# Two transformer blocks in one fp32 kernel: the opening stage and the first norm put into one block, with two of four modulation blocks as products on TensorE

## The chip, the cores and the metric

## What is computed

Two transformer blocks run one behind the other on a sequence of 512 tokens of width 1024; the second has 256 context tokens beside them. Only the opening matters here:

```python
c_act = jax.nn.silu(c)
mod = (c_act @ w_ada[l] + b_ada[l])[:, None, :]           # 1 x 1024 times 1024 x 6144
sh_m, sc_m, ga_m, sh_f, sc_f, ga_f = jnp.split(mod, 6, axis=-1)
h = _rms_norm(x, g_pre_mix[l]) * (1.0 + sc_m) + sh_m
y = _hybrid_mixer(h, ...)                                 # opens with proj = h @ w_in

def _rms_norm(x, g):
    y = xf * lax.rsqrt(jnp.mean(xf * xf, axis=-1, keepdims=True) + EPS)
    return (y * g).astype(x.dtype)
```

The first norm needs the shift `sh_m` and the scale `sc_m`, the first 2048 of the 6144 columns: four blocks of 512, numbered 0 to 3.

## The kernel before

`build` runs five stages in turn. Instructions are written out by hand for each engine in blocks (`nc.Block()`), each engine runs its list in the order in which it is written, and a block ends with a barrier of all engines. Within a block, semaphores alone order the engines.

Activations are held with the features on the 128 partitions: `K.x[:, k, ...]` is feature group k of 8 (`KT`), with 256 context tokens and then 512 tokens. Weights come through `K.ring`, three slots of 2 MB, in a fixed order (`weight_items`): the w_ada blocks 0, 1, 2, 3, then the query weights (`nq`, eight pieces), the key weights (`kv`), and so on. SP issues the load of an item once the item three places before has been left, that is, once the semaphore named in `ring.left` has its value.

**`stage_start`** loads constants, tokens and context on SP's queue and 20 rows of small parameters on ACT's. PE turns the parameters (line 393), then the tokens and the context in alternation, 8 feature groups each (line 402; four transposes for the tokens, two for the context), into four banks. DVE copies every bank to `K.x` (line 344). Then come the four modulation blocks: `modulation_sums` on DVE multiplies each of 8 tiles of 128x512 weights by its column of silu(c) and adds (lines 439 and 441), which leaves one 128x512 tile of partial sums; `modulation_columns` on PE adds over the partitions, with 128 columns of that tile as the stationary side and a column of ones moving (line 467), four matmuls a block, straight into the columns of bank 7 in which the rest wants them. Lines 349 and 352 on DVE make shift and scale.

**`rms_norms`**, called at the top of `stage_mixer_1`, is a block of its own: ACT loads its table and squares the 8 groups (line 500) into two buffers, PE sums each over the partitions with a matrix of ones (line 523), ACT takes Ln and Exp (lines 505, 506), DVE multiplies by the root (line 542) into two buffers, and ACT applies scale and shift (line 512) to give `K.h`.

**`project_1`** is the next block. PE multiplies `K.h` by the query weights (line 823), with the sums for the context's norm (line 832) and rotations (line 796) between; SP loads first three halves of the second block's modulation weights and then the next item of the ring.

## Time and profile before

| | |
|---|---|
| median of 3 runs | 2465.08 us (2464.07 to 2465.39) |
| profiled execution, its time | 2464.89 us |
| profiled execution, its span | 2463.1 us |
| PE busy, share of the span | 2300.7 us, 93% |
| DVE busy | 1036.7 us, 42% |
| ACT busy | 484.0 us, 20% |
| POOL busy | 693.3 us, 28% |
| DMA, mean over the span | 102 GB/s |

The span is what the trace covers, from the first instruction to the last; the profiled execution's own time is 1.8 us more. Times in the trace count from the start of the span. The granted clock is 1.00 at 2.4 GHz and 0.50 at 1.2 GHz. A row of the timeline may stand for several instructions (x8): its duration then runs from the first one's start to the last one's end.

### The profile page before, as it was taken

The numbers are of one execution on the slowest core, as the hardware profiler recorded it, in microseconds if no ns is written. First come the engines' busy times: TensorE is split into PE (matmuls) and PEld (weight loads), VectorE is DVE, ScalarE is ACT, GpSimd is POOL, SyncE is SP. The second block draws the span as 40 slices with busy tenths as digits, with TensorE's granted clock in tenths as the row PEclk, the third lists the DMA queues.
The fourth block names the chain that finished last, engine by engine and source line by source line (L and its number), as shares of the span: only waits on it lengthen the run. The fifth ranks groups of instructions, "written<-read, shape, count | busy, mean of one in ns | idle before, by whom it ended". The sixth has DMA issues, their size and how long they took to land. (4 is left out here: it accounts for less than half of the span.)

```text
span 2463.1 us, 26565 instructions
## 1 busy us (share of the span) xinstructions
PE 2300.7 (93%) x10463; PEld 1790.6 (73%) x10463; DVE 1036.7 (42%) x1913; ACT 484.0 (20%) x1110; POOL 693.3 (28%) x549
## 2 busy tenths in 40 slices
PE   4899897889999899999989999997999899999998
PEld 2454576667776788888878888885556668888887
DVE  5555386443342763235453322452433422112354
ACT  1201122223342200101130011113132532000002
POOL 0000000000001355556245555640010103555552
PEclk7999697889999999999989999998999999999999
DMA  8632432543341245223234522231121121222230
GB/s 278 207 112 103 135 103 74 181 143 95 95 138 51 86 157 185 74 66 93 94 102 137 186 88 71 71 116 44 34 73 69 35 69 43 95 91 70 71 93 36
DMA packets 255271, 250.14 MB, mean 102 GB/s; under 512 B 19858, under 2 KB 207404, under 8 KB 255020
## 3 DMA queue, kind: packets, MB, share of 16 engines
q1 hardware_dynamic: 254712, 248.30, 32.1%
q8 instruction: 84, 1.38, 0.2%
q14 instruction: 39, 0.32, 0.0%
q10 hardware_dynamic: 436, 0.15, 0.0%
HBM read 243.19 MB, written 4.19 MB: 100 GB/s over the span
## 5 line engine op out<-in xcount | busy, mean ns | idle before, releaser
L1917 POOL TENSOR_TENSOR w_sums<-ring 128x512 f32<-128x512 f32 x66 | 91.7, 1389 | 528.5 <-POOLq L1249 355.7
L1933 POOL TENSOR_TENSOR hidden<-rstd,h_act 128x256 f32<-128x256 f32 x66 | 53.9, 816 | 434.6 <-DVE h_act L2110 434.6
L823 PE MATMUL ps<-h_act,ring 128*128 128x512 f32 (+1 forms) x288 | 129.7, 605 | 9.5 <-PEq L487 8.7
L1802 PE MATMUL ps<-h_sums,w_sums 128*128 128x256 f32 x528 | 128.5, 387 | 10.6 <-DVE h_sums L2046 10.6
L2110 DVE TENSOR_TENSOR h_act<-ps,rstd 128x256 f32<-128x256 f32 x78 | 33.0, 424 | 233.2 <-PE ps L1820 136.6
L1820 PE MATMUL ps<-h_sums,ring 128*128 128x256 f32 x528 | 125.8, 381 | 3.1 <-DVE rstd L2089 3.1
L1808 PE MATMUL ps<-h_act,ring 128*128 128x256 f32 x528 | 126.9, 384 | 0.0
L1767 PE MATMUL ps<-h_act,ring 128*128 128x256 f32 x528 | 125.2, 381 | 0.0
L1814 PE MATMUL ps<-h_sums,w_sums 128*128 128x256 f32 x528 | 124.8, 379 | 0.2 <-DVE rstd L2082 0.2
L1825 PE MATMUL ps<-h_act,w_sums 128*128 128x256 f32 x528 | 124.7, 379 | 0.0
L1775 PE MATMUL ps<-h_act,ring 128*128 128x256 f32 x528 | 124.5, 379 | 0.0
L2082 DVE TENSOR_TENSOR rstd<-ps,h_act 128x256 f32<-128x256 f32 x78 | 33.1, 425 | 212.5 <-PE ps L1802 176.1
L1802 PEld LDWEIGHTS ps<-h_sums,w_sums 128*128 128x128 f32 x528 | 102.2, 194 | 26.0 <-issue 11.7
L1615 PE MATMUL ps<-h_act,ring 128*128 128x256 f32 (+1 forms) x384 | 113.3, 455 | 4.5 <-PEq L2452 3.9
L1820 PEld LDWEIGHTS ps<-h_sums,ring 128*128 128x128 f32 x528 | 99.5, 190 | 20.3 <-DVE rstd L2089 7.2
L1808 PEld LDWEIGHTS ps<-h_act,ring 128*128 128x128 f32 x528 | 102.1, 193 | 14.5
L1814 PEld LDWEIGHTS ps<-h_sums,w_sums 128*128 128x128 f32 x528 | 100.2, 190 | 14.2 <-DVE rstd L2082 0.6
L1775 PEld LDWEIGHTS ps<-h_act,ring 128*128 128x128 f32 x528 | 100.1, 190 | 14.3 <-issue 0.8
L1825 PEld LDWEIGHTS ps<-h_act,w_sums 128*128 128x128 f32 x528 | 100.3, 190 | 13.6
L823 PEld LDWEIGHTS ps<-h_act,ring 128*128 128x128 f32 (+1 forms) x288 | 53.8, 189 | 77.5 <-issue 77.2
L1767 PEld LDWEIGHTS ps<-h_act,ring 128*128 128x128 f32 x528 | 99.4, 190 | 13.0
L1615 PEld LDWEIGHTS ps<-h_act,ring 128*128 128x128 f32 x384 | 73.4, 192 | 42.0 <-issue 35.3
(443 smaller groups left out, 4456.3 us busy)
## 6 DMA issues: line engine op xcount, KB each, us to landing
ring<-in_ffn_w_in SPq DMA_DIRECT2D x66, 1024.0 KB, 7.7
ring<-in_w_ada SPq DMA_DIRECT2D x12, 2048.0 KB, 8.5
ring<-in_w_mod SPq DMA_DIRECT2D x12, 2048.0 KB, 8.0
ring<-in_w_gate_up SPq DMA_DIRECT2D x22, 1024.0 KB, 8.1
ring<-in_ffn_w_out SPq DMA_DIRECT2D x32, 704.0 KB, 5.8
ring<-in_w_in SPq DMA_DIRECT2D x6, 2048.0 KB, 8.1
ring<-in_ffn_w_out SPq DMA_DIRECT2D x8, 1408.0 KB, 7.1
ring<-in_w_down SPq DMA_DIRECT2D x16, 704.0 KB, 6.4
```

Of the source, the lines that this page charges most:

```text
L823: last = pe.matmul(K.ps[i % 3][0:rows, :], lhs(w, item, j, k), hl(k), start=(k == 0), stop=(k == KT - 1))
L1615: last = pe.matmul(K.ps[i % 3][:, 0:b - a], w[:, k, (d % 4) * P:(d % 4) * P + P], K.h[:, k, CTX + a:CTX + b], start=(k == 0), stop=(k == K ...
L1767: last = pe.matmul(pa, a11[:, k], F.h11[:, k], start=(k == 0), stop=(k == 3))
L1775: last = pe.matmul(pa, a12[:, k], F.h21[:, k], start=False, stop=(k == 3), skip_group_check=True)
L1802: last = pe.matmul(pb, s2[:, k], F.t2[:, k], start=(k == 0), stop=(k == 3))
L1808: last = pe.matmul(pc, a21[:, k], F.h12[:, k], start=(k == 0), stop=(k == 3))
L1814: last = pe.matmul(pb, s1[:, k], F.t1[:, k], start=(k == 0), stop=(k == 3))
L1820: last = pe.matmul(pc, a22[:, k], F.t4[:, k], start=False, stop=(k == 3), skip_group_check=True)
L1825: last = pe.matmul(pb, s4[:, k], F.h22[:, k], start=False, stop=(k == 3), skip_group_check=True)
L1917: pool.tensor_tensor(s1, a21, a22, ALU.add).then_inc(S["wsum"].sem, 1)
L1933: pool.tensor_tensor(one[:, j], F.gate1[f % 2], F.got21[f % 2], ALU.mult)
L2082: dve.tensor_tensor(F.v, pb, F.kept1[u % 2], ALU.add).then_inc(S["v"].sem, 1)
```

## The change

`stage_start` and the first norm become one block, and `rms_norms` with its helpers goes.

- SP loads the tokens in two halves, then modulation block 0, then the context.
- PE turns the tokens alone, then sums the squares for the norm, then turns the context. DVE copies the turned tokens as before; ACT copies the context.
- ACT squares each group of `K.x` as soon as it is copied. Ln and Exp follow the sums.
- Blocks 1 and 3 are products on PE (`product`): the column of silu(c) is the stationary side, 128x1, the weights 128x512 are the moving side, 8 matmuls add up one row of 512. ACT copies the row to SBUF, and four matmuls with one partition (`columns`) turn it into columns. Blocks 0 and 2 stay with DVE.
- DVE multiplies `K.x` by the root into `K.h` between its two blocks; ACT applies scale and shift in place.
- The counts of `K.mod_mm` follow, since only two blocks now pass through it (`MODS_START`). In later stages some semaphores are shared (`K.out_mm`) or left out where nothing uses them. Apart from the names of these semaphores the order on every engine behind this block is as before, and POOL's list does not change.

PE behind the last block of columns, before. `sq` is the tile that DVE leaves, `ones` a matrix of ones, line 523 the sum of the squares, line 823 the first projection:

```order
L467 MATMUL ps<-ones,sq 128x1 [waits mod_sum]
L467 MATMUL ps<-ones,sq 128x1 x3
L327 UNCONDITIONAL_BRANCH
L516 UNCONDITIONAL_BRANCH [waits barrier_Pool_Activation_PE_DVE_SP_release]
L523 MATMUL ps<-sq,ones 128x512 [waits norm_sq] x8
L487 UNCONDITIONAL_BRANCH
L787 UNCONDITIONAL_BRANCH [waits barrier_Pool_Activation_PE_DVE_SP_release]
L823 MATMUL ps<-h_act,ring 128x512 [waits ring_filled1]
```

After, PE from the end of the context's transposes to the last columns. `cc` is silu(c); `rstd` and `sq` hold the copied rows in line 429; line 533 is `modulation_columns`:

```order
L421 MATMUL ps<-ring,cc 1x512 [waits ring_filled1,silu_done]
L421 MATMUL ps<-ring,cc 1x512 x7
L533 MATMUL ps<-ones,sq 128x1 [waits mod_sum]
L533 MATMUL ps<-ones,sq 128x1 x3
L429 MATMUL ps<-ones,rstd 128x1 [waits st_row_kept]
L429 MATMUL ps<-ones,rstd 128x1 x3
L421 MATMUL ps<-ring,cc 1x512 [waits ring_filled0]
L421 MATMUL ps<-ring,cc 1x512 x7
L429 MATMUL ps<-ones,sq 128x1 [waits st_row_kept]
L429 MATMUL ps<-ones,sq 128x1 x3
L533 MATMUL ps<-ones,sq 128x1 [waits mod_sum]
L533 MATMUL ps<-ones,sq 128x1 x3
```

Two barriers between columns and projection have become one, the sums of the squares have moved ahead (they stand before the context's transposes), and two products stand between the columns, the second queued behind the columns of the first.

DVE from the fourth modulation block to the norm's multiplications, before:

```order
L439 TENSOR_SCALAR sq<-ring,cc 128x512 [waits mod_mm,ring_filled0]
L441 SCALAR_TENSOR_TENSOR sq<-ring,cc,sq 128x512 [waits dve_step] x7
L349 TENSOR_TENSOR mod<-ps,par 128x16 [waits mod_mm]
L352 SCALAR_TENSOR_TENSOR coef<-mod,par 128x8 [waits x_kept]
L327 UNCONDITIONAL_BRANCH
L526 UNCONDITIONAL_BRANCH [waits barrier_Pool_Activation_PE_DVE_SP_release]
L542 TENSOR_TENSOR tmp<-x_res,rstd 128x512 [waits norm_std]
L542 TENSOR_TENSOR tmp<-x_res,rstd 128x512
L542 TENSOR_TENSOR tmp<-x_res,rstd 128x512 [waits norm_out] x6
```

After, DVE from the copies of the tokens to the coefficients:

```order
L346 COPY x_res<-ps 128x512 [waits x_turned] x8
L505 TENSOR_SCALAR sq<-ring,cc 128x512 [waits ring_filled0,silu_done]
L507 SCALAR_TENSOR_TENSOR sq<-ring,cc,sq 128x512 [waits dve_step] x7
L351 TENSOR_TENSOR h_act<-x_res,rstd 128x512 [waits st_root]
L351 TENSOR_TENSOR h_act<-x_res,rstd 128x512 x7
L505 TENSOR_SCALAR sq<-ring,cc 128x512 [waits ring_filled2]
L507 SCALAR_TENSOR_TENSOR sq<-ring,cc,sq 128x512 [waits dve_step] x7
L355 TENSOR_TENSOR mod<-ps,par 128x16 [waits mod_mm,st_row_cols]
L358 SCALAR_TENSOR_TENSOR coef<-mod,par 128x8 [waits st_coef]
```

Two of the four sums are gone, the context's copies are gone, the multiplications by the root stand between the two sums that are left, and the coefficients wait for `st_row_cols` as well.

```diff
@@ -72,6 +72,7 @@
+MODS_START = 2
...
@@ -317,9 +319,13 @@
-    const_in, param_in, x_in = K.sem("const_in"), K.sem("param_in"), K.sem("x_in")
+    const_in, param_in, x_in = K.sem("const_in"), K.sem("param_in"), [K.sem(f"x_in{i}") for i in range(3)]
     set_done, par_t, par_done = K.sem("set_done"), K.sem("par_t"), K.sem("par_done")
-    turned, kept, silu_done = K.sem("x_turned"), K.sem("x_kept"), K.sem("silu_done")
+    turned, kept, ctx_kept, silu_done = K.sem("x_turned"), K.sem("x_kept"), K.sem("ctx_kept"), K.sem("silu_done")
+    squared, summed, log, root, normed, row_mm, row_kept, row_cols, coef = (K.sem(f"st_{n}") for n in (
+        "squared", "summed", "log", "root", "normed", "row_mm", "row_kept", "row_cols", "coef"))
+    rows = [K.rstd[0:1, 1, :], K.sq[0:1, 0, :]]
+    rstd = K.rstd[:, 0, :]
     with ExitStack() as st:
...
@@ -335,22 +341,22 @@
                 for g in range(3):
                     dve.wait_ge(par_t, g + 1)
                     dve.tensor_copy(K.par[g][:, :], K.ps[g][:, 0:PCOL[g]]).then_inc(par_done, 1)
-                for k in range(0, KT):
-                    for part in range(2):
-                        i = 2 * k + part
-                        dve.wait_ge(turned, i + 1)
-                        dst = K.x[:, k, CTX:TOK] if part == 0 else K.x[:, k, 0:CTX]
-                        src = K.ps[3 + i % 4][:, 0:SEQ if part == 0 else CTX]
-                        dve.tensor_copy(dst, src).then_inc(kept, 1)
+                for k in range(KT):
+                    dve.wait_ge(turned, k + 1)
+                    dve.tensor_copy(K.x[:, k, CTX:TOK], K.ps[3 + k % 4][:, :]).then_inc(kept, 1)
                 dve.wait_ge(silu_done, 1)
-                for n in range(4):
-                    modulation_sums(K, dve, ("ada", n))
-                dve.wait_ge(K.mod_mm, 4)
-                dve.tensor_tensor(K.mod1[:, 0:16], K.ps[7][:, 0:16], K.p("b_ada", 0, 16), ALU.add).then_inc(kept, 1)
-                dve.wait_ge(kept, 2 * KT + 1)
+                modulation_sums(K, dve, ("ada", 0))
+                dve.wait_ge(root, 1)
+                for k in range(KT):
+                    dve.tensor_tensor(K.h[:, k, CTX:TOK], K.x[:, k, CTX:TOK], rstd, ALU.mult).then_inc(normed, 1)
+                modulation_sums(K, dve, ("ada", 2))
+                dve.wait_ge(row_cols, 2)
+                dve.wait_ge(K.mod_mm, 2)
+                dve.tensor_tensor(K.mod1[:, 0:16], K.ps[7][:, 0:16], K.p("b_ada", 0, 16), ALU.add).then_inc(coef, 1)
+                dve.wait_ge(coef, 1)

                 dve.scalar_tensor_tensor(K.coef[:, 0], K.mod1[:, 8:16], 1.0, K.p("g_pre_mix"), ALU.add,
-                                         ALU.mult).then_inc(kept, 1)
+                                         ALU.mult).then_inc(coef, 1)

             @block.scalar
             def _(act):
@@ -383,33 +389,93 @@
                 act.activation(K.cc1[:, :], K.p("c"), ACT.Silu)
                 act.activation(K.cc2[:, :, 0], K.p("c_2"), ACT.Silu)
                 act.activation(K.cc2[:, :, 1], K.p("c_ctx_2"), ACT.Silu).then_inc(silu_done, 1)
+                act.preload_act_table_set(LOG_EXP)
+                for k in range(KT):
+                    act.wait_ge(kept, k + 1)
+                    if k >= 2:
+                        act.wait_ge(summed, k - 1)
+                    act.activation(K.tmp[:, k % 2, :], K.x[:, k, CTX:TOK], ACT.Square).then_inc(squared, 1)
+                act.wait_ge(summed, KT)
+                act.activation(rstd, K.ps[0][:, :], ACT.Ln, bias=K.eps[:, 0:1], scale=1.0 / D).then_inc(log, 1)
+                act.wait_ge(log, 1)
+                act.activation(rstd, rstd, ACT.Exp, scale=-0.5).then_inc(root, 1)
+                for k in range(KT):
+                    act.wait_ge(turned, KT + k + 1)
+                    act.activation(K.x[:, k, 0:CTX], K.ps[3 + k % 4][:, 0:CTX], ACT.Copy).then_inc(ctx_kept, 1)
+                for i in range(2):
+                    act.wait_ge(row_mm, i + 1)
+                    if i == 1:
+                        act.wait_ge(K.mod_mm, 1)
+                    act.activation(rows[i], K.ps[1 + i][0:1, :], ACT.Copy).then_inc(row_kept, 1)
+                act.wait_ge(coef, 2)
+                act.wait_ge(normed, KT)
+                for k in range(KT):
+                    h = K.h[:, k, CTX:TOK]
+                    act.activation(h, h, ACT.Identity, bias=K.mod1[:, k:k + 1], scale=K.coef[:, 0, k:k + 1])

             @block.tensor
             def _(pe):
+                def product(n, i):
+                    w = K.ring.take(pe, ("ada", n)).rearrange("p (k n) -> p k n", k=KT)
+                    for k in range(KT):
+                        last = pe.matmul(K.ps[1 + i][0:1, :], K.cc1[:, k:k + 1], w[:, k, :], start=(k == 0),
+                                         stop=(k == KT - 1))
+                    last.then_inc(row_mm, 1)
+                    K.ring.left(row_mm, i + 1)
+
+                def columns(n, i):
+                    pe.wait_ge(row_kept, i + 1)
+                    for c in range(4):
+                        last = pe.matmul(K.ps[7][:, 4 * n + c:4 * n + c + 1], rows[i][:, c * P:c * P + P],
+                                         K.ones[0:1, 0:1], start=True, stop=True)
+                    last.then_inc(row_cols, 1)
+
                 pe.wait_ge(const_in, 16)
                 pe.wait_ge(param_in, 16 * n_params)
                 for g in range(3):
                     n = PCOL[g]
                     pe.transpose(K.ps[g][:, 0:n], prow[0:n, g, :], const(K, "ident")[0:n, 0:n]).then_inc(par_t, 1)
-                pe.wait_ge(x_in, 32)
+                pe.wait_ge(x_in[0], 16)
+                pe.wait_ge(x_in[1], 16)
                 for k in range(KT):
-                    for part in range(2):
-                        i = 2 * k + part
-                        if i >= 4:
-                            pe.wait_ge(kept, i - 3)
-                        src = xr if part == 0 else cr
-                        for t in range(QT if part == 0 else CC):
-                            last = pe.transpose(K.ps[3 + i % 4][:, t * P:t * P + P], src[:, t, k * P:k * P + P],
-                                                const(K, "ident"))
-                        last.then_inc(turned, 1)
-                for n in range(4):
-                    modulation_columns(K, pe, ("ada", n))
+                    if k >= 4:
+                        pe.wait_ge(kept, k - 3)
+                    for t in range(QT):
+                        last = pe.transpose(K.ps[3 + k % 4][:, t * P:t * P + P], xr[:, t, k * P:k * P + P],
+                                            const(K, "ident"))
+                    last.then_inc(turned, 1)
+                pe.wait_ge(set_done, 1)
+                pe.wait_ge(par_done, 3)
+                for k in range(KT):
+                    pe.wait_ge(squared, k + 1)
+                    pe.matmul(K.ps[0][:, :], K.ones[:, :], K.tmp[:, k % 2, :], start=(k == 0),
+                              stop=(k == KT - 1)).then_inc(summed, 1)
+                pe.wait_ge(x_in[2], 16)
+                for k in range(KT):
+                    if k < 4:
+                        pe.wait_ge(kept, 5 + k)
+                    else:
+                        pe.wait_ge(ctx_kept, k - 3)
+                    for t in range(CC):
+                        last = pe.transpose(K.ps[3 + k % 4][:, t * P:t * P + P], cr[:, t, k * P:k * P + P],
+                                            const(K, "ident"))
+                    last.then_inc(turned, 1)
+                pe.wait_ge(silu_done, 1)
+                product(1, 0)
+                modulation_columns(K, pe, ("ada", 0))
+                columns(1, 0)
+                product(3, 1)
+                columns(3, 1)
+                modulation_columns(K, pe, ("ada", 2))

             @block.sync
             def _(sp):
                 sp.dma_start(K.cst[:, :], A["consts"]).then_inc(const_in, 16)
-                sp.dma_start(xr[:, :, :], A["x"][0].rearrange("(t p) d -> p t d", p=P)).then_inc(x_in, 16)
-                sp.dma_start(cr[:, :, :], A["ctx_2"][0].rearrange("(t p) d -> p t d", p=P)).then_inc(x_in, 16)
+                x = A["x"][0].rearrange("(t p) d -> p t d", p=P)
+                for i in range(2):
+                    sp.dma_start(xr[:, 2 * i:2 * i + 2, :], x[:, 2 * i:2 * i + 2, :]).then_inc(x_in[i], 16)
+                K.ring.load_ahead(sp, ("ada", 0))
+                sp.dma_start(cr[:, :, :], A["ctx_2"][0].rearrange("(t p) d -> p t d", p=P)).then_inc(x_in[2], 16)
                 K.ring.load_ahead(sp, "kv")

...
@@ -470,97 +536,11 @@
-def rms_norms(K, jobs):
...
 def stage_mixer_1(K, out):
-    rms_norms(K, [norm_in(lat(K.x), SEQ, K.coef[:, 0], K.mod1[:, 0:8], lat(K.h))])
...
@@ -904,14 +884,14 @@
-                    dve.wait_ge(K.mod_mm, 4 + 4)
+                    dve.wait_ge(K.mod_mm, MODS_START + 4)
...
@@ -1592,7 +1572,7 @@
-    O.mm = K.sem(f"po_mm{call}")
+    O.mm = Tally(K.out_mm, call * len(OUT_PIECES))
```

## Rows read from the trace of the kernel before

**Rows 1.** Timeline: start us, us, engine line op; in brackets idle before and releaser

```profile
14.29 1.11 PE L402 MATMUL ps<-cst,x_rows 128*128 128x128 f32 x4 [0.26 <-DMA ctx_rows<-in_ctx]
...
15.44 1.02 DVE L344 COPY x_res<-ps 128x512 f32<-128x512 f32 x2 [1.16 <-PE ps L402]
...
16.90 0.87 PE L402 MATMUL ps<-cst,x_rows 128*128 128x128 f32 x4
...
17.82 0.60 PE L402 MATMUL ps<-cst,x_rows 128*128 128x128 f32 x4
...
21.83 0.38 PE L402 MATMUL ps<-cst,ctx_rows 128*128 128x128 f32 x2
...
23.91 5.48 DVE L441 SCALAR_TENSOR_TENSOR sq<-ring,cc,sq 128x512 f32<-128x512 f32 x7
```

**Rows 2.** Timeline, the four modulation blocks and the coefficients

```profile
29.30 0.48 DVE L439 TENSOR_SCALAR sq<-ring,cc 128x512 f32<-128x512 f32 x1
...
35.32 10.07 SPq L237 DMA_DIRECT2D ring<-in_w_in  x10
...
47.16 1.86 PE L467 MATMUL ps<-ones,sq 128*128 128x1 f32 x8 [4.04 <-DVE sq L441]
...
49.27 0.17 DVE L352 SCALAR_TENSOR_TENSOR coef<-mod,par 128x8 f32<-128x8 f32 x1
```

**Rows 3.** Timeline, the norm and the start of the first projection

```profile
51.70 9.13 PE L523 MATMUL ps<-sq,ones 128*128 128x512 f32 x16 [2.68 <-ACT sq L500]
...
58.04 0.63 ACT L500 ACTIVATE sq<-x_res 128x512 f32<-128x512 f32 x1 [0.23 <-PE ps L523]
...
59.03 0.63 ACT L500 ACTIVATE sq<-x_res 128x512 f32<-128x512 f32 x1 [0.35 <-PE ps L523]
...
60.87 0.69 ACT L505 ACTIVATE rstd<-ps,eps 128x512 f32<-128x512 f32 x1 [1.22 <-PE ps L523]
...
62.98 6.24 ACT L512 ACTIVATE h_act<-tmp,mod,coef 128x512 f32<-128x512 f32 x8 [0.76 <-DVE tmp L542]
...
69.52 10.06 PE L823 MATMUL ps<-h_act,ring 128*128 128x512 f32 x16 [8.69 <-PEq L487]
```

**Rows 4.** Timeline of PE later in the first projection

```profile
178.47 0.28 PE L467 MATMUL ps<-ones,sq 128*128 128x1 f32 x2
...
180.17 7.11 PE L823 MATMUL ps<-h_act,ring 128*128 128x512 f32 x16
...
230.16 7.04 PE L823 MATMUL ps<-h_act,ring 128*16 128x512 f32 x16
```

**Rows 5.** Windows: us, busy of each engine (records), PEclk (granted clock), DMA share, GB/s

```profile
24.00:26.00 2.00, 0.00 (x0) 0.00 (x0) 1.93 (x3) 0.00 (x0) 0.00 (x0) 0.57 1.06 389
...
54.00:56.00 2.00, 2.00 (x4) 0.48 (x2) 0.00 (x0) 1.07 (x2) 0.00 (x0) 0.75 0.00 0
...
230.00:237.20 7.20, 7.20 (x20) 1.68 (x19) 4.19 (x7) 0.00 (x0) 0.00 (x0) 1.00 0.69 262
...
257.00:273.00 16.00, 15.77 (x16) 4.00 (x16) 4.10 (x6) 1.88 (x4) 0.00 (x0) 0.50 0.94 269
...
283.20:286.60 3.40, 3.40 (x34) 3.40 (x32) 2.49 (x4) 0.00 (x0) 0.00 (x0) 1.00 0.00 0
...
286.60:290.00 3.40, 3.40 (x20) 3.40 (x20) 0.16 (x1) 0.31 (x1) 0.00 (x0) 0.57 0.89 287
```

**Rows 6.** Groups by form: line engine op shapes xcount, busy us, mean ns, idle before

```profile
L344 DVE COPY x_res<-ps 128x512 f32<-128x512 f32 x8 | 5.5, 688 | 1.5 <-PE ps L402 1.4
...
L542 DVE TENSOR_TENSOR tmp<-x_res,rstd 128x512 f32<-128x512 f32 x8 | 5.4, 691 | 13.5 <-ACT rstd L506 12.8 <-ACT h_act L512 0.6
...
L684 ACT ACTIVATE rstd<-ps 128x256 f32<-128x256 f32 x8 | 3.1, 383 | 24.6 <-PE ps L645 24.6
```

**Rows 7.** Line 237, the loads of the ring, issued in 29 to 35 us

```profile
L237 SPq DMA_DIRECT2D ring<-in_w_ada x1: 368/368/368, 29.4 to 29.4; - x1
...
DMA to landing us min/median/max: 8.0/8.0/8.0
```

More of the change, by code:

```diff
@@ L292, in build @@
         K.mods_summed = K.mods_turned = 0
-        K.norm_sems = {n: Tally(nc.alloc_semaphore(f"norm_{n}")) for n in ("sq", "mm", "std", "tmp", "out")}
+        K.norm_sems = {n: Tally(nc.alloc_semaphore(f"norm_{n}")) for n in ("sq", "mm", "std", "tmp")}
+        K.out_mm = nc.alloc_semaphore("out_mm")
         K.fast = {n: nc.alloc_semaphore(f"fast_{n}") for n in FAST_COUNTS}
@@ L1400, in coefs_1 @@
 def coefs_1(K, dve, done):
[L1402 removed]
+    dve.wait_ge(K.mod_mm, MODS_START + 8 + MODS_FIRST)
     dve.tensor_tensor(K.mod1[:, 16:48], K.ps[7][:, 16:48], K.p("b_ada", 16, 32), ALU.add).then_inc(done, 1)
@@ L1417, in coefs_2 @@
     m = K.ps[7][:, 48:192].rearrange("p (j v) -> p j v", v=2)
-    dve.wait_ge(K.mod_mm, 12 + MODS_FFN[call][-1] + 1)
+    dve.wait_ge(K.mod_mm, MODS_START + 8 + MODS_FFN[call][-1] + 1)
     n = 0
@@ L1616, in out_tensor @@
                              start=(k == 0), stop=(k == KT - 1))
-        last.then_inc(O.mm, 1)
+        last.then_inc(O.mm.sem, 1)
         if i in (3, len(OUT_PIECES) - 1):
-            K.ring.left(O.mm, i + 1)
+            K.ring.left(O.mm.sem, O.mm.base + i + 1)
         if O.context and i < 4:
@@ L1644, in out_scalar @@
     for i, (d, a, b, _) in enumerate(OUT_PIECES):
-        act.wait_ge(O.mm, i + 1)
+        O.mm.wait(act, i + 1)
         y_square(K, O.T, act, i, K.ps[i % 3][:, 0:b - a])
```

74 lines of the change are left out of this document (3 added, 71 removed).

## The prediction, made before the changed kernel was run

> **What bounds the kernel now.** I read the timeline of the first 70 us first, because the change ends there: the order of the instructions after the first projection is the same on every engine, so whatever the first projection gains in its start is the whole gain, unless the clock at that start differs. The reader should see three things. First, DVE is the bound from 15.4 us on: it copies the turned tokens and then sums four blocks of w_ada back to back, 5.9 us each (three of them from 29.30 to the 47.16 at which PE gets the last) [rows 1, 2], while PE only turns each finished sum into columns (1.86 us) and ACT is idle. Second, the tail is serial: last columns end 49.02, coefficients end 49.44 [rows 2]. Third, the norm starts only then, although its squares need nothing but x, which was in place before 23.9: squares and their sums on PE to 60.83, Ln and Exp to 62.22 (the 62.98 less the 0.76 of idle), then eight scalings on ACT to 69.22, and the first projection matmul at 69.52 [rows 3]. That is 20.1 us behind the coefficients, of which only the last 6.24 depend on them.
>
> **What the change removes, and the new chain.** I build the new start of the projection, T', from rows, and compare it with 69.52. Every engine is followed; PE turns out last.
>
> 1. Tokens alone are turned now: PE starts at 14.03 (the 14.29 less the 0.26 it waited for the context) [rows 1]. At first twelve transposes take 14.29 to 16.90, 0.87 for a group of four; at the fast level a group is done in 0.60 with its drain (17.82) [rows 1]. DVE's copy is 0.69 [rows 6] and starts 1.15 behind the first transpose: 15.2. The third copy waits for PE until 14.03 + 3 x 0.87 + 0.3 = 16.95, the rest run back to back at 0.70, so the fourth ends 18.35 and the eighth 21.15. PE's last group reuses the bank of the fourth copy and ends between 18.8 and 18.95; I take 18.8, since the sum follows while it drains.
> 2. The sum over the features: 8 matmuls. Fast, the square loop steps by 0.86 to 0.99 (58.04 and 59.03; the floor is 7.04 / 8 = 0.88) [rows 3, 4]; I take 0.93, 7.4 in all: 26.2. The squares on ACT come earlier: they follow the copies, and the table load ahead of them falls into ACT's idle time.
> 3. Ln and Exp: 60.83 to 62.22, 1.4 [rows 3]: 27.6. The second table load and one block boundary of the old path are gone.
> 4. The context is turned behind the sums. Four groups go at once, the other four wait for ACT, which copies 0.38 each [rows 6] from 27.6: 27.6 + 4 x 0.38 + 0.25 = 29.4.
> 5. First product (block 1) on PE. The trace has no matmul with one stationary column. The nearest row has 16 of them and 512 moving: 8 matmuls (16 records) in 7.04, the same as with 128 [rows 4]. Since eight times fewer columns saved nothing, 7.0 is the lower end; the upper is twice that, 14.1, at the slow level. I take 7.0, the value of the nearest row: 36.4. Its weights are there: DVE began on them at 29.30 without a wait [rows 2], and the bytes queued ahead of them are unchanged.
> 6. Columns of block 0 and then of the product, four matmuls each. At the fast level eight such took 1.70 (178.47 to 180.17), at the slow one four took 1.86 [rows 2, 4]. Two sets: 1.7, 38.1. The copy of the row on ACT (0.69 as the Ln of a bank, the dearest of its kind) lies beside the first set. The products' columns have one partition as stationary depth, which no row has; bounds 0.8 and 1.9 a set.
> 7. Second product 7.0: 45.1. Its weights are issued when DVE has summed block 0 (21.15 + 5.9 = 27.05) and took 8.0 to land [rows 7]: 35.1, wanted at 38.1. That cover is 3.0.
> 8. Here nothing hides the row's copy: 0.7, then two sets 1.7: 47.5. Block 2, which DVE summed, is queued behind the second product's columns.
> 9. The two small operations for the coefficients: 49.02 to 49.44, 0.4: 47.9.
> 10. Eight scalings 6.24 and the boundary 0.30 (69.22 to 69.52) [rows 3]: 54.45. For some eight handoffs between engines, 0.02 to 0.05 each, I add 0.4: **T' = 54.9**.
>
> The other engines are early: DVE multiplies by the root eight times at 0.69 [rows 6] from 27.6 to 33.2, sums block 2 to 39.1, and PE asks for it at 46.7. On SP the query weights wait for the first product, now 36.4 instead of 35.3; all ten issues, the keys' included, take 10.1 [rows 2], and even the 8.0 of a 2 MB load behind the last gives 54.5 [rows 7]; the query's pieces are the first eight, so they are in before 54.9. Splitting the load of x in two and putting block 0 ahead of the context change no byte that PE waits for before 14.03; the context is wanted at 26.2 and was there at 14.29 [rows 1]; with 2 MB more ahead of it, it comes at most 8.0 later [rows 7]. Renamed semaphores and shared counters cost nothing.
>
> So the projection starts 69.52 - 54.9 = 14.6 earlier. Its own first group ran slow, 10.06 against 7.04 [rows 3, 4], behind 8.7 of idle PE; now PE idles 7.4 before it, and I expect the same 3.0 to be lost (if the level stayed high instead, 3.0 more would be gained). The profiled execution of 2464.89 then becomes 2450.3; the median of the runs is 0.2 above it: **2450.4**.
>
> **A rule against the change.** Of transposes the rows show that four took 1.11 at first and 0.60 from 17.82 on, though nothing but transposes had run since 14.29 [rows 1]: PE reached its fast level on them. The Trainium skill (TensorE: Matmul & The Clock Gate, Part 4: PE-mode transpose) says that the full clock does not engage in transpose mode, since it does not count as PE-busy in the same way. By that rule the sums would open at the slow level. Worked out from rows, that mechanism gives: transposes at 0.87 a group to 21.0, the sums in 9.13 as they took after an idle PE [rows 3], ending 30.1 instead of 26.2, so 2454.3. The trace disagrees with the rule, so it gets little.
>
> **Rivals.** All hang on the level of PE's clock, since 24.8 us of the new chain (sums 7.4, products 14.0, columns 3.4) are PE work that doubles at 1.2 GHz, where before DVE's sums did not care.
>
> *The level falls in the context gap* (26.2 to 29.4, where PE has 16 transposes and an idle stretch of 0.9). For: after the last transposes at 21.83 the granted clock fell, 0.57 from 24 to 26 [rows 1, 5]. Against: there the idle stretch went on, here it is short, and the last transposes before, each pair held up by DVE's copies, still took 0.38 for two [rows 1]. Price: 1.7 (9.13 less 7.4 for the sums) to 3.0 (first projection group) [rows 3, 4]: 2452.1 to 2453.4, say 2452.8.
>
> *One stationary column does not hold the level.* For: a busy PE is not enough. Matmuls of one moving column kept it busy 3.40 of 3.40 and the level fell right behind, 1.00 to 0.57; and with 16 of 128 rows in every second matmul PE was busy 15.77 of 16.00 and stayed at 0.50 [rows 5]. Against: 16 stationary columns, busy for 7.04, held 1.00 through 230.0 to 237.2 [rows 5]; the moving side there is as full as in the products. Price: product 29.4 to 43.5, two sets 3.7, product to 61.3, copy 0.7, two sets to 65.7, then 0.4, 6.24, 0.3 and 0.4: T' = 73.1. That would be 2468.5; with the first of it still fast, 2466.8. I put it at 2468.
>
> *The slow level from the first transpose to the last column*, the case on the other side. Transposes to 21.0, sums 14.1 to 35.1, 8.9 later than forecast, then the products as above: T' = 82.0, 2477. It decides from the point where 14.6 of the 24.8 us of PE work are lost; for 0.2% beyond, 19.5. Against: in the kernel before these same sums, from 51.70 on, raised the level by themselves: 0.75 over 54 to 56 [rows 3, 5].
>
> **How the numbers follow.** Forecast 0.56; level lost in the gap 0.23; transposes as by the rule 0.03; products slow 0.14; slow throughout 0.04. The range takes in the first three (0.82): down to 2447.4 if the projection opens fast, up to 2456 for the rule's case with the higher bounds of the columns and handoffs. A measurement of this kernel tells about 0.2%, 4.9 us, from no change: faster (below 2460.1) is the first three, 0.82; same holds the products at the slow level, 0.14; slower 0.04.
>
> **What would show it.** In the profile after: sums start near 18.8 and end near 26.2; each product has 16 records of 0.59 (1.1 if slow) and lasts 7.0; granted clock 1.00 from 17 to 47; the scalings start near 48 and follow the last columns, not DVE; the first projection matmul is at 54.9, with its first group near 10.1. I am wrong if a window between 26 and 47 shows 0.50, if PE waits for block 3 at 38, or if the projection waits for its weights.

## The result, and the profile after

The changed kernel took 2445.7 us (median of 4 runs, 2443.27 to 2448.42) beside 2464.57 us of the kernel before on the same chip: a ratio of 0.9927, 95% interval 0.9913 to 0.9942. It is faster by 18.9 us, where 14.6 was forecast, and the median lies 1.7 us below the low end of the range. The profiled execution took 2447.78 us, its span is 2446.0.

The timeline of the start (start us, duration us, engine, line, operation, tiles, count; in brackets the idle time before and what ended it) answers to [rows 1 to 3]:

```profile
13.66 5.51 PE L444 MATMUL ps<-cst,x_rows 128*128 128x128 f32 x32
...
17.37 3.08 DVE L346 COPY x_res<-ps 128x512 f32<-128x512 f32 x5 [0.16 <-PE ps L444]
19.01 7.61 PE L451 MATMUL ps<-tmp,ones 128*128 128x512 f32 x16
...
26.66 0.69 ACT L399 ACTIVATE rstd<-ps,eps 128x512 f32<-128x512 f32 x1 [1.22 <-PE ps L451]
...
28.33 1.26 PE L460 MATMUL ps<-cst,ctx_rows 128*128 128x128 f32 x8 [0.84 <-ACT x_res L404]
...
29.52 7.03 PE L421 MATMUL ps<-ring,cc 128*1 128x512 f32 x16
...
36.48 1.05 PE L533 MATMUL ps<-ones,sq 128*128 128x1 f32 x8
...
37.46 1.05 PE L429 MATMUL ps<-ones,rstd 1*128 1x1 f32 x8
...
38.44 7.03 PE L421 MATMUL ps<-ring,cc 128*1 128x512 f32 x16
...
45.51 0.59 ACT L409 ACTIVATE sq<-ps 1x512 f32<-1x512 f32 x1 [8.33 <-PE ps L421]
...
48.28 0.17 DVE L355 TENSOR_TENSOR mod<-ps,par 128x16 f32<-128x16 f32 x1 [9.43 <-PE ps L533]
48.49 0.17 DVE L358 SCALAR_TENSOR_TENSOR coef<-mod,par 128x8 f32<-128x8 f32 x1
48.69 5.74 ACT L414 ACTIVATE h_act<-h_act,mod,coef 128x512 f32<-128x512 f32 x8 [2.60 <-DVE coef L358]
...
54.73 8.90 PE L803 MATMUL ps<-h_act,ring 128*128 128x512 f32 x16 [6.56 <-PEq L333]
...
63.90 7.03 PE L803 MATMUL ps<-h_act,ring 128*128 128x512 f32 x16
```

PE now carries the block: it has work nearly without a gap from 13.66 to 48.17, and DVE, the bound of before, waits 9.4 us for it ahead of the coefficients. The norm's root is there at 28.0, 20 us before the coefficients. Windows of the same stretch (busy time of PE, PEld, DVE, ACT, POOL with the number of records, then granted clock, DMA share, GB/s) show the clock that the prediction hung on:

```profile
17.00:26.00 9.00, 9.00 (x33) 4.38 (x32) 8.59 (x14) 3.80 (x7) 0.00 (x0) 1.00 1.04 396
26.00:30.00 4.00, 3.16 (x20) 1.87 (x19) 2.32 (x5) 3.31 (x10) 0.00 (x0) 1.00 1.05 387
30.00:36.00 6.00, 6.00 (x16) 1.13 (x14) 5.86 (x10) 0.20 (x1) 0.00 (x0) 1.00 0.89 326
...
45.00:48.00 3.00, 2.32 (x18) 1.84 (x16) 0.00 (x0) 0.59 (x1) 0.00 (x0) 1.00 1.28 240
48.00:50.00 2.00, 0.17 (x2) 0.09 (x1) 0.34 (x2) 1.31 (x2) 0.00 (x0) 0.53 1.05 369
```

The granted clock is 1.00 (2.4 GHz) from the transposes to the last columns, through the context gap of 26 to 30 too; in this profile it falls to 1.2 GHz only where PE waits for the scalings, 0.53 and then 0.50.

So the projection starts at 54.73 instead of 69.52 [rows 3], 14.8 earlier. But the spans differ by 2463.1 - 2446.0 = 17.1, and the medians by 18.9. The experiments ask two things: whether the start gained for the reasons given, and where the rest comes from.

### The profile page after: what moved, and what is told of

The parts are those of the page before. It is cut to its first block and busy times, and to the rows that moved or that the text cites. A ratio compares the mean times of both kernels' runs of the same rounds, so it can differ in the third digit from the quotient of the medians.

```text
span 2446.0 us, 26616 instructions
## 1 busy us (share of the span) xinstructions
PE 2311.3 (94%) x10495; PEld 1793.0 (73%) x10495; DVE 1022.4 (42%) x1889; ACT 487.1 (20%) x1120; POOL 689.9 (28%) x549
## 5 line engine op out<-in xcount | busy, mean ns | idle before, releaser
L1782 PEld LDWEIGHTS ps<-h_sums,w_sums 128*128 128x128 f32 x528 | 103.3, 196 | 26.4 <-issue 11.7
L1800 PEld LDWEIGHTS ps<-h_sums,ring 128*128 128x128 f32 x528 | 99.5, 190 | 19.5 <-DVE rstd L2069 6.4
L1788 PEld LDWEIGHTS ps<-h_act,ring 128*128 128x128 f32 x528 | 102.9, 195 | 14.9
```

Of the source, the lines that this page charges most:

```text
L1782: last = pe.matmul(pb, s2[:, k], F.t2[:, k], start=(k == 0), stop=(k == 3))
L1788: last = pe.matmul(pc, a21[:, k], F.h12[:, k], start=(k == 0), stop=(k == 3))
L1800: last = pe.matmul(pc, a22[:, k], F.t4[:, k], start=False, stop=(k == 3), skip_group_check=True)
```

## The experiments

Two theories about the rest. By the first, the gain at the start is passed on rigidly, and what is beyond it is the scatter of single runs. By the second, moving the start changes where behind it the clock falls and rises, and this gives or takes a few microseconds by itself. All comparisons are with the kernel before on the same chip.

**One half alone: the norm beside the transposes, all four blocks summed on DVE.** From the changed kernel, `product(1, 0)` and its like are left out of PE's program and DVE sums all blocks:

```diff
                 for k in range(KT):
                     dve.tensor_tensor(K.h[:, k, CTX:TOK], K.x[:, k, CTX:TOK], rstd, ALU.mult).then_inc(normed, 1)
-                modulation_sums(K, dve, ("ada", 2))
+                for n in range(1, 4):
+                    modulation_sums(K, dve, ("ada", n))
...
```

> The changed kernel with all four modulation blocks summed on VectorE, none as a product; the norm stays in the block. By the rows of the changed kernel: block 0 is summed by 26.3, the multiplications by the root end 32.9, three more sums of 5.95 end 50.7, columns at the slow level 1.9, coefficients 0.45, scalings 5.75 and boundary 0.3: projection at 59.1. If the rival is right that the merged norm alone brings the gain and the products nothing, it starts at 54.7. Forecast 59.1, time 4.4 above the changed kernel's, less than the spread of single runs.

Measured: 2455.79 us (8 runs), ratio 0.9960, interval 0.9946 to 0.9973; mean 2454.0. Its timeline:

```profile
50.74 1.87 PE L524 MATMUL ps<-ones,sq 128*128 128x1 f32 x8 [4.04 <-DVE sq L498]
...
53.06 5.74 ACT L409 ACTIVATE h_act<-h_act,mod,coef 128x512 f32<-128x512 f32 x8 [22.84 <-DVE coef L358]
...
59.10 10.16 PE L794 MATMUL ps<-h_act,ring 128*128 128x512 f32 x16 [6.49 <-PEq L333]
```

PE gets the last sum 3.6 later than before (47.16, [rows 2]), since DVE now also multiplies by the root. But nothing stands behind the coefficients but the scalings: the projection starts 10.4 earlier. The idle time of 4.04 ahead of the columns says that DVE is still the bound. The start of 59.10 is the one forecast, and the rival by which the products bring nothing falls with it; the time is not: the mean is 9.1 us above the changed kernel's, where 4.4 was expected.

**The other half alone: two products on PE, the norm where it was.** The same two products and their columns, in the old block:

```diff
-                for n in range(4):
-                    modulation_sums(K, dve, ("ada", n))
-                dve.wait_ge(K.mod_mm, 4)
+                modulation_sums(K, dve, ("ada", 0))
+                modulation_sums(K, dve, ("ada", 2))
+                dve.wait_ge(row_cols, 2)
+                dve.wait_ge(K.mod_mm, 2)
...
+                product(1, 0)
+                modulation_columns(K, pe, ("ada", 0))
+                columns(1, 0)
+                product(3, 1)
+                columns(3, 1)
+                modulation_columns(K, pe, ("ada", 2))
```

> The kernel before, norm in its own block, with blocks 1 and 3 as products on TensorE. The first product starts near 25, just as the clock falls: 10 to 14 us; the second cannot start before block 3 has landed at 37.4, ends 44.5 at the fast level, columns and coefficients by 47.5; then the old norm, 20.1: projection at 67.6, a gain of 2 out of the 14.8. If products and merged norm add up, it would be 14.8 - 10.4 = 4.4.

Measured: 2461.51 us (12 runs), ratio 0.9986, interval 0.9976 to 0.9997; mean 2461.2. That is at most a small gain. Its timeline shows where it goes:

```profile
25.26 8.72 PE L402 MATMUL ps<-ring,cc 128*1 128x512 f32 x16 [2.58 <-DMA ring<-in_w_ada]
29.87 0.37 SPq L238 DMA_DIRECT2D ring<-in_w_ada  x1
...
37.99 7.03 PE L402 MATMUL ps<-ring,cc 128*1 128x512 f32 x16 [2.05 <-DMA ring<-in_w_ada]
...
50.46 10.36 PE L555 MATMUL ps<-sq,ones 128*128 128x512 f32 x16 [2.73 <-ACT sq L532]
...
60.86 0.69 ACT L537 ACTIVATE rstd<-ps,eps 128x512 f32<-128x512 f32 x1 [1.22 <-PE ps L555]
...
69.52 9.10 PE L850 MATMUL ps<-h_act,ring 128*128 128x512 f32 x16 [8.70 <-PEq L519]
```

PE waits for weights twice, 2.58 for block 1 and 2.05 for block 3, which is issued only at 29.87, when DVE has given its part of the ring back. The sums of the squares start 1.2 earlier than in [rows 3] and take 10.36 instead of 9.13, with more of them at the slow level, so that the Ln stands where it stood, at 60.86 against 60.87. Products alone are hidden behind the weights and the clock. The gain of 2 at the start that was expected is 0.0 against [rows 3] (69.52 both times), and 1.1 if taken at the second group of matmuls (78.88 against 80.0, the mean of two profiles of the kernel before); the first product took 8.72, less than the 10 to 14 expected. Beside the early norm they bring 4.4 at the start of the projection (59.10 to 54.73), and 9.1 in the means (2454.0 to 2444.9, the mean of all runs of the changed kernel below).

**A product that opens cold.** The first product is made to wait until DVE has finished its second sum (`pe.wait_ge(K.mod_sum, 2)` ahead of `product(1, 0)`), so that PE stands idle for 9.4 us ahead of it:

> The changed kernel in which TensorE waits for VectorE's second sum (38.8) ahead of its first product, so that it is idle from 29.5 on and the clock falls. Does a matmul with one stationary column count? If it does not raise the level, the first product takes 14.1 and the second too, and the projection starts at about 80. If it does, the first takes 9 to 11, the second 7.0, and the projection starts at 54.7 + 9.4 + 3 = 67.

Measured: 2455.75 us, in a single run. Timeline and windows:

```profile
39.43 8.58 PE L421 MATMUL ps<-ring,cc 128*1 128x512 f32 x16 [9.36 <-issue]
...
49.90 7.03 PE L421 MATMUL ps<-ring,cc 128*1 128x512 f32 x16
```

```profile
38.00:40.00 2.00, 0.57 (x1) 0.11 (x2) 1.29 (x2) 0.00 (x0) 0.00 (x0) 0.50 0.00 0
40.00:42.00 2.00, 2.00 (x4) 0.30 (x3) 0.00 (x0) 0.00 (x0) 0.00 (x0) 0.50 0.04 8
42.00:44.00 2.00, 2.00 (x6) 0.34 (x5) 0.00 (x0) 0.00 (x0) 0.00 (x0) 0.86 0.00 0
44.00:48.00 4.00, 4.00 (x11) 0.72 (x9) 0.00 (x0) 0.00 (x0) 0.00 (x0) 1.00 0.00 0
```

The product starts at 0.50 and raises the clock itself, to 0.86 and then 1.00; the cold start cost it 1.55 (8.58 less 7.03), and the projection starts at 66.19, near the 67 of that case and far from the 80 of the other. One stationary column is enough here, both to hold and to raise the level. The first product of the kernel with the products alone says the same from a second run: 8.72 behind 2.58 of idle PE. The rival by which one column is not enough falls.

**Dummy work to hold the level.** Seven matmuls whose result nobody reads, behind the last columns of the changed kernel:

```diff
                 columns(3, 1)
                 modulation_columns(K, pe, ("ada", 2))
+                for k in range(7):
+                    pe.matmul(K.ps[0][:, :], K.ones[:, :], K.x[:, k, CTX:TOK], start=True, stop=True)
```

> The changed kernel with seven matmuls of 128x512 more on TensorE (ones times x, result unused) behind its last columns, 48.2 to about 54.2, where it was idle. The projection still starts at 54.7. R, with the clock's price taken at the start alone: the granted clock stays 1.00, the first group takes 7.1 instead of 8.9, span 2446.0 - 1.8 = 2444.2. S: the same first group, but the end moves by 0 or by 3 to 4 us, not by 1.8.

Measured: 2446.03 us (6 runs), ratio 0.9932, interval 0.9918 to 0.9946; mean 2445.6.

```profile
48.52 7.95 PE L471 MATMUL ps<-x_res,ones 128*128 128x512 f32 x14
...
56.77 7.11 PE L805 MATMUL ps<-h_act,ring 128*128 128x512 f32 x16 [0.30 <-PEq L333]
```

The first group takes 7.11 instead of 8.90: its loss does come from the idle PE ahead. But the seven took 7.95, not the 6.2 of the fast level (14 records of 0.44), and end 1.6 behind the scalings (56.47, 54.92). The projection starts 2.0 later than in the changed kernel, about what its group is shorter by. The expectation had it start at 54.7 still, and a span of 2444.2 or one moved by 0 or by 3 to 4 us; the profile's span is 2443.3 and the mean 0.7 above the changed kernel's. Nothing is won.

**The start moved by known amounts.** In the kernel before, four squarings on ACT that nobody reads are put at the end of the norm (2.3 us); in the changed kernel, two and four of them (1.15 and 2.3 us) behind the last scaling, here the four:

```diff
+            for dst in (K.sq[:, 0, :], K.sq[:, 1, :], K.rstd[:, 1, :]):
+                act.activation(dst, K.rstd[:, 0, :], ACT.Square)
+            act.activation(K.h[:, 0:2, 0:CTX], K.rstd[:, 0, :].rearrange("p (a n) -> p a n", a=2), ACT.Square)
```

```diff
+                for dst in (K.tmp[:, 0, :], K.tmp[:, 1, :], K.sq[:, 0, :], K.sq[:, 1, :]):
+                    act.activation(dst, rstd, ACT.Square)
```

> The kernel before, with four squarings of 128x512 more on ScalarE behind the norm's last scaling, 2.3 us in all, results unused; the first projection starts at 71.8 instead of 69.5. Theory R (everything behind the projection's start shifts rigidly): span 2463.1 + 2.3 = 2465.4. Theory S (the end is set by where the later falls and rises of TensorE's clock come, and work re-aligns to them): in the two traces these changes stand 17.07 us apart from 1220 us on, though the projection started only 14.8 earlier; so the first 2.3 us of that start are free, the span stays at 2463.1 within 0.5.

> The changed kernel with two squarings more on ScalarE behind the last scaling, 1.15 us; the projection starts at 55.9. R: span 2446.0 + 1.2 = 2447.2. S: the start lies then, against the clock's changes, as it did in the kernel before, so its first group of matmuls takes 10.1 again instead of 8.9 and the span is 3 to 4 us longer than 2446.0, not 1.2.

> The same with four squarings, 2.3 us; the projection starts at 57.0. R: span 2448.3. S: no more than with two, since work re-aligns to the same clock changes: equal to the run with two squarings within 0.5.

Measured: before with 2.3 more 2461.58 (12 runs; ratio 1.0001, 0.9988 to 1.0014; mean 2463.0); after with 1.15 more 2446.09 (6 runs; 0.9933, 0.9918 to 0.9949; mean 2445.9); after with 2.3 more 2443.68 (6 runs; 0.9925, 0.9909 to 0.9940; mean 2443.8). The profiles show the starts at 72.64, 56.19 and 56.72, which is 3.1, 1.5 and 2.0 later than in the first profile of each kernel. Passed on rigidly, that gives +2.3, +1.15 and +2.3. Measured, mean against mean: +0.2 (the kernel before had 2462.8 on that chip), +1.0 and -1.1 (against the 2444.9 of all runs of the changed kernel). The second theory had named 0 for the first of them, which fits, 3 to 4 for the middle one, and for the last the same as for the middle one: it misses both. The first theory misses the first by 2.1 and the last by 3.4, and fits the middle one. Each kernel's runs spread by 7 to 12 us, so that a mean of 6 is good to 2 or 3 us only: these runs exclude neither theory, and the question was put below what so few runs resolve.

**Both kernels once more.**

> The changed kernel, unedited, for more runs beside more of the kernel before. The runs so far spread over 10 us for either kernel, and a delay of 1.15 or 2.3 us did not show in their times. Theory N (the start of the projection moves by 14.8, the rest of the difference is where in each run the clock's changes fall): means apart by 14.8, within 1.5. Theory G (something behind the projection's start became faster for good): 17 or more.

> The changed kernel once more, to enlarge the sample beside the kernel before on the same chip: the mean of ten runs so far is 2445.4 against 2463.8 of the kernel before in forty, a difference of 18.3, where the projection starts 14.8 earlier. Theory N (only the start counts, the rest is the spread of the runs): the pooled difference moves toward 15 to 17. Theory G (something behind the start gives more): it stays at 18 or above.

> The kernel before once more, for a second profile of it. The changed kernel's three profiles start the projection at 54.73, 54.44 and 54.95 and its second group at 63.90, 64.8 and 64.21, so the start hardly varies, while their spans are 2446.0, 2437.7 and 2443.0. If the kernel before behaves likewise, its projection starts within 0.5 of 69.52 and its second group between 78.6 and 79.9, and what lies behind the second group varies by several us with the amount of slow level in it: the 191.5 us at the slow level behind the start that its first profile has would be found changed by 10 or more. If instead its start varies by 2 or 3, the forecast of 14.6 was anchored on a chance start, and the 3 us between the gain at the start and the gain in the mean would come from there.

Measured: the changed kernel 2445.54 (6 runs; ratio 0.9921, 0.9904 to 0.9938) and 2443.95 (6 runs; 0.9916, 0.9899 to 0.9933); the kernel before against itself 0.9999 (0.9983 to 1.0014), with runs from 2454.33 to 2469.69 us. Taken together: before 2463.4 in the mean of 80 runs (they spread with a standard deviation of 3.8), after 2444.9 in the mean of 16 (2.8): a difference of 18.5, with 1.6 of uncertainty at 95%. By the words of the two expectations for the changed kernel that is the case of something behind the start that gives more: 19.5 in the first repetition, where 14.8 within 1.5 stood against 17 or more, and 18.5 with the second, where 15 to 17 stood against 18 or above. How much more depends on what is taken for the gain at the start. The timeline of the kernel before, second profile:

```profile
52.54 9.85 PE L523 MATMUL ps<-sq,ones 128*128 128x512 f32 x16 [2.68 <-ACT sq L500]
...
71.08 8.84 PE L823 MATMUL ps<-h_act,ring 128*128 128x512 f32 x16 [8.69 <-PEq L487]
...
80.19 5.31 PE L823 MATMUL ps<-h_act,ring 128*128 128x512 f32 x12
```

What was expected of this second profile came out in neither form. The start of the projection is 1.6 later than in [rows 3], 71.08, but its first group is 1.2 shorter; the second group starts at 80.19, where 79.85 stood in the first profile. In three profiles of the changed kernel it starts at 63.90, 64.79 and 64.21. By the second groups the gain at the start is 80.0 - 64.3 = 15.7, with a scatter of 0.9 at most in either kernel. The slow level behind the start, from 90 us on, was 191.5 us in the first profile of before and is 194.9 in the second, so it did not change by the 10 or more that were expected; in the three of after it is 201.7, 177.8 and 191.5. More scatter lies behind. Two profiles of the same changed kernel, spans 2446.0 and 2437.7: in the first, an instruction on ACT that both have stands at 448.88 and a later one at 812.92,

```profile
448.88 0.38 ACT L677 ACTIVATE x_res<-ps 128x256 f32<-128x256 f32 x1 [2.61 <-PE ps L616]
...
812.92 0.42 ACT L1984 ACTIVATE h_act<-h_act 128x256 f32<-128x256 f32 x1 [13.49 <-DVE h_act L2103]
```

and in the second (a run of the same program) they stand at

```profile
445.41 0.38 ACT L677 ACTIVATE x_res<-ps 128x256 f32<-128x256 f32 x1 [1.66 <-PE ps L616]
...
804.96 0.42 ACT L1984 ACTIVATE h_act<-h_act 128x256 f32<-128x256 f32 x1 [12.56 <-DVE h_act L2103]
```

3.5 and then 8.0 us earlier, though the second had started its second group of matmuls 0.9 later. One group of PE in that stretch and windows around two short waits of PE, in the first profile:

```profile
783.72 6.22 PE L1518 MATMUL ps<-hidden,ones 128*128 128x256 f32 x16 [3.90 <-ACT hidden L1511]
...
780.00:790.00 10.00, 6.29 (x18) 5.14 (x19) 5.98 (x6) 4.96 (x9) 0.00 (x0) 0.66 0.32 103
796.00:806.00 10.00, 6.46 (x18) 4.96 (x17) 5.63 (x6) 3.40 (x6) 0.00 (x0) 0.66 0.01 2
```

and in the second, the same group and windows around the same two waits:

```profile
779.18 3.72 PE L1518 MATMUL ps<-hidden,ones 128*128 128x256 f32 x16 [3.90 <-ACT hidden L1511]
...
774.00:784.00 10.00, 6.10 (x28) 5.05 (x28) 7.01 (x7) 6.58 (x13) 0.00 (x0) 1.00 0.47 154
789.00:799.00 10.00, 6.43 (x23) 5.06 (x22) 5.71 (x7) 3.37 (x6) 0.00 (x0) 0.83 0.00 0
```

The granted clock is the third number from the right: 0.66 and 0.66 in the one, 1.00 and 0.83 in the other. The same 16 records behind the same 3.90 of idle PE take 6.22 in the one and 3.72 in the other: the clock falls in one run and not, or for less time, in the other. The runs' mean clocks go with their times: 0.957 and 0.958 at spans of 2446.0 and 2446.6, 0.962 at 2439.3 and 2439.7 (changed kernel); and in 29 runs of the kernel before on one chip 0.959 or 0.960 in the four below 2456 us, 0.951 to 0.953 in the eight of 2466 us and more.

**Can it be made faster still.** The profile of after says what is serial at the end: the second product's row copy (0.59), the columns of block 2 behind it, and eight scalings on ACT while DVE idles. The next kernel turns block 2 first and gives five of the scalings to DVE; the one after it adds three dummy matmuls behind the last columns:

```diff
                 dve.wait_ge(coef, 2)
+                dve.wait_ge(normed, KT)
+                for k in range(3, KT):
+                    h = K.h[:, k, CTX:TOK]
+                    dve.tensor_scalar(h, h, K.coef[:, 0, k:k + 1], K.mod1[:, k:k + 1], ALU.mult, ALU.add)
...
-                for k in range(KT):
+                for k in range(3):
...
                 product(3, 1)
-                columns(3, 1)
                 modulation_columns(K, pe, ("ada", 2))
+                columns(3, 1)
+                for k in range(3):
+                    pe.matmul(K.ps[0][:, :], K.ones[:, :], K.x[:, k, CTX:TOK], start=True, stop=True)
```

> The changed kernel with two more edits at the end of its first block: PE turns DVE's sum of block 2 into columns while ACT copies the second product's row, and the last scalings are shared, three on ACT and five on DVE, in place of eight on ACT. If the profile of the changed kernel is read rightly, the 0.6 of the row's copy is hidden and five scalings of 0.48 each on DVE take the place of 5.74 on ACT: the last columns end near 47.5, the coefficients near 48.0, the first projection matmul starts near 50.7 in place of 54.73, 4.0 earlier. Theory N (a start moved by so much moves the mean of many runs by so much, give or take what the clock gives back in the first group, where PE idles less): mean 4.0 less than the changed kernel, near 2441. Theory G (a gain at the start is partly given back or enlarged behind, by where the clock changes fall): the profile shows the 4.0 at the start, and the mean of the runs stands off 2441 by more than 2.

> The previous kernel with three matmuls of 512 moving columns whose result nobody reads behind the last columns, so that PE works through part of the 3.3 in which it would wait for the scalings. If the level of the first projection's first group hangs on that idle time, the group takes 7.1 to 8 in place of 8.9 to 10.1, and the mean is up to 2.5 less than that of the previous kernel, near 2439. If the level has already fallen because of the matmuls of one moving column ahead, the three run slow (5 to 5.2 in all), the projection starts some 1.5 to 2 late, and the time is equal or 1 worse.

Measured: with the shared scalings 2440.21 us (5 runs), ratio 0.9905, interval 0.9889 to 0.9921, mean 2441.1; with the dummy matmuls too 2437.10 us (5 runs), ratio 0.9891, interval 0.9875 to 0.9907, mean 2437.7. The first one's timeline:

```profile
46.26 1.05 PE L538 MATMUL ps<-ones,sq 128*128 128x1 f32 x8
46.36 0.59 ACT L414 ACTIVATE sq<-ps 1x512 f32<-1x512 f32 x1 [8.33 <-PE ps L426]
...
48.73 2.23 ACT L419 ACTIVATE h_act<-h_act,mod,coef 128x512 f32<-128x512 f32 x3 [1.79 <-DVE coef L358]
48.73 2.37 DVE L364 TENSOR_SCALAR h_act<-h_act,coef,mod 128x512 f32<-128x512 f32 x5
...
51.41 9.77 PE L808 MATMUL ps<-h_act,ring 128*128 128x512 f32 x16 [3.12 <-PEq L333]
```

and the second one's:

```profile
46.99 4.54 PE L476 MATMUL ps<-x_res,ones 128*128 128x512 f32 x6
...
51.83 7.11 PE L810 MATMUL ps<-h_act,ring 128*128 128x512 f32 x16 [0.30 <-PEq L333]
```

The row's copy now lies beside the columns of block 2, and 2.37 of scalings stand where 5.74 stood. The projection starts 3.3 earlier than at 54.73, not the 4.0 expected, because this profile's second product starts 0.9 later (its 32 transposes took 6.46, not 5.51); from the second product on, the start is 4.2 nearer. The mean, 2441.1, is the one that the first theory had named, but five runs don't settle it. The dummies took 4.54 in place of 2.7, slowed as in the experiment with seven, and end 1.6 behind the scalings (49.88, 51.5), but the first group pays that back with 2.7 (9.77 to 7.11): so the slow dummies of the one branch of the expectation came with the fast group of the other. In the two profiles the second groups start 2.3 apart (61.45 and 59.20); 1.2 of it was there before the dummies (the second product at 39.30 and 38.07), and 1.0 is the dummies' net. The 3.4 between the two means of five runs each is uncertain by 3.0 at 95%, so it doesn't say more than that. Against the changed kernel's mean of 2444.9 the last version is 7 us better, and it is the fastest kernel of this study.

## Why the prediction was wrong, and what of it was right

The mechanism at the start came out as forecast; what failed is the step from that start to the time of the whole kernel, and with it the low end of the range, by 1.7.

**The bound and the chain: right, step by step.** Forecast and measured: PE starts 14.03, 13.66; the eighth copy ends 21.15, 20.45; sums end 26.2, 26.6; root 27.6, 28.0; product start 29.4, 29.5; product 7.0, 7.03 and ends 36.4, 36.55; second product starts 38.1, 38.4 and ends 45.1, 45.5; last columns 47.5, 48.2; coefficients 47.9, 48.7; T' 54.9 against 54.73, 54.44 and 54.95 in three profiles. That T' came out within 0.5 is in part luck: two terms were off and cancelled. A set of columns takes 1.05 with its drain, where 0.85 was taken; this holds for the one-partition sets too, whose bounds were 0.8 and 1.9. The eight scalings take 5.74, not 6.24: in [rows 3] each pair waited a little for DVE's multiplication (the 6.24 had those waits in it), and now DVE is done long before.

**The one price without a row: right, and by the nearest row.** The products were costed at 7.0 with 14.1 as the other end. In the experiment with the cold product the second product took 7.03 again, and the first, from the slow level, 8.58.

**The clock: right.** The gap of 26 to 30 kept 1.00, so the rival with 0.23 did not happen; nor did the slow products or the slow start. The sums opened at full speed right behind transposes, 7.61 for 16 records. The Trainium skill (TensorE: Matmul & The Clock Gate, Part 4: PE-mode transpose) would have had them open slow; here the trace disagrees again.

**The weights: right in the outcome, off in a term.** Block 3 landed later than the 8.0 of [rows 7]:

```profile
L238 SPq DMA_DIRECT2D ring<-in_w_ada x1: 368/368/368, 26.4 to 26.4; - x1
...
DMA to landing us min/median/max: 10.7/10.7/10.7
```

26.4 + 10.7 = 37.1, wanted at 38.44. The cover was 1.3, not 3.0. In the kernel with the products alone, where block 3 was issued at 29.87, there was none, and PE waited 2.05.

**What failed: the step from the start to the time.** The prediction said that "whatever the first projection gains in its start is the whole gain, unless the clock at that start differs", took the loss of the first group as the same 3.0, and anchored on one profiled execution. Against the mean of 16 runs (2444.9), 2450.4 is 5.5 too high, in three terms:

- The first group. It lost 3.0 in the profile of before, 1.8 in its second one, and 1.9, 3.0 and 2.0 in the three of after. By the second groups the gain is 15.7 instead of 14.6: 1.1.
- The base. The three runs shown lay at 2464.07 to 2465.39; 80 runs spread from 2454.33 to 2469.69 with a mean of 2463.4: 1.7.
- What lies behind the second group: 2.8 (18.5 in the means less 15.7). Its uncertainty is 1.6 from the means alone, over half of it, and more with that of the starts.

The range is where this became an error. Its low end, 2447.4, came from one event at the start (the projection opening fast), while each trace of this kernel has some twenty stretches at 1.2 GHz, some of them at short waits where another run of the same kernel has none, and the runs of one kernel differed by 3 to 15 us. A median of four runs moves by a microsecond or two for that reason alone, at both kernels. None of it was in the sum, because three runs within 1.3 us of each other were taken for the spread.

**What stays open: the last 2.8.** For each kernel, the gain in the mean less the gain by the start of the second group (80.0 and 2463.4 as base): norm alone 9.4 - 10.5 = -1.1; products alone 2.2 - 1.1 = +1.1; the changed kernel +2.8; with seven dummies 17.8 - 15.9 = +1.9; with 1.15 and 2.3 more 17.5 - 14.9 = +2.6 and 19.6 - 13.5 = +6.1; shared scalings 22.3 - 18.6 = +3.7; with three dummies 25.7 - 20.8 = +4.9; before with 2.3 more 0.4 + 2.3 = +2.7. Most are positive, and they don't grow in step with the gain. That something behind the start gives back 2 to 4 us to these kernels is likely by this list, but not shown. It is hardly the later semaphores of the change: the norm-alone kernel has all of them, and -1.1. Nor is it the total of the slow level alone: with the same 191.5 us of it from 90 us on, the stretch behind the second group's start took 2383.3 in the kernel before, but 2378.8 in the changed one (third profile) and 2379.6 with the shared scalings. What it is stays open, since two profiles of one kernel differ by 9 us in the same stretch. An answer would need traces of many runs of each kernel, not one or three.

## What to carry to other kernels

Ask of each statistic of a norm what it needs: the squares need only the input, so they can be taken while weights still arrive, and only the last scaling belongs behind the coefficients; that half of the change, with the context's copies moved to ACT and one barrier less, was 9 or 10 of the 18 us here. Work that moves to another engine is worth what the chain behind it lets through: the two products brought 1 to 2 us by themselves, hidden behind weights and the norm, and 5 by the second group beside the early norm (69.52 to 64.3). And before a range is drawn from one profile, look at how often the clock falls in it: whether it falls behind a short wait differs from run to run, and three runs that agree don't show it.

## What the runs showed of the hardware

- A matmul of f32 with one stationary column and 512 moving ones costs what one with 128 costs, 7.03 for 16 records, and it raised the clock from 1.2 to 2.4 GHz (8.58 from a cold start) and held it (1.00 from 30 to 45).
- A busy PE does not always hold it. Dummy matmuls right behind the last 2.0 us of columns with one moving element started fast and slowed within, 7.95 for 14 records (6.2 at the fast level) and 4.54 for 6 (2.7), though PE had no idle time from the columns on. Two such sets between the two products, 2.0 us too, did not make it fall: 1.00 from 30 to 45.
- The same kernel on one chip varied by 15 us in 29 runs (2454.33 to 2469.69), and the longer runs had the lower mean clock. Two profiles of one program show the clock fall around a short wait of PE in one run and not in the other (0.66 against 1.00 over 10 us; 6.22 against 3.72 for the same 16 records).
- The first group of the projection cost 8.90, 10.08 and 8.99 in place of 7.03 in three profiles of one program, behind the same 6.6 of idle PE; and 10.06 and 8.84 in two of the kernel before, behind 8.7.
- The load of block 3 took 10.7 to land, where it took 8.0 before; why was not tried.
